# Eight of the 22 feature tiles of both down projections as Strassen block products

## The reference

```python
def swiglu(x, w_gate, w_up, w_down):
    return (jax.nn.silu(x @ w_gate) * (x @ w_up)) @ w_down

h = x + 0.5 * rmsnorm(swiglu(rmsnorm(h, ffn1_pre_g), ...), ffn1_post_g)
h = h + rmsnorm(hybrid_mixer(rmsnorm(h, mix_pre_g), ...), mix_post_g)
h = h + 0.5 * rmsnorm(swiglu(rmsnorm(h, ffn2_pre_g), ...), ffn2_post_g)
```

## Time and profile before

| | |
|---|---|
| median of 3 runs | 1090.79 us (1090.13 to 1091.5) |
| profiled execution, its own time | 1090.27 us |
| its span on the core | 1088.4 us, mean granted TensorE clock 1.000 |
| busy share of the span | PE 99%, DVE 61%, ACT 46%, POOL 4% |
| moved by DMA | 121.17 MB, mean 111 GB/s |

### The profile page before, as it was taken

One profiled execution on the slowest core, in us unless ns is written; L12 is line 12 of the kernel. 1 busy time (PEld: TensorE's weight loads), 2 busy tenths in 40 slices (PEclk: granted clock), 3 DMA queues, 4 the chain that ended last, 5 costly groups with the idle time before them and its releaser, 6 DMA issues.

```text
span 1088.4 us, 15986 instructions
## 1 busy us (share of the span) xinstructions
PE 1075.5 (99%) x6534; PEld 957.5 (88%) x6534; DVE 667.9 (61%) x810; ACT 503.0 (46%) x729; POOL 44.7 (4%) x96
## 2 busy tenths in 40 slices
PE   8999999999999999999999999999999999999997
PEld 6899999998888978888888888889899999988886
DVE  6898888873334663476664333468687887753334
ACT  7354455552223573667773222344445454542222
POOL 2000000000001210001000000011000000000001
PEclk9999999999999999999999999999999999999999
DMA  9522423334322544332115334315434234153311
GB/s 301 183 78 87 147 79 101 133 98 174 96 81 58 175 121 108 84 78 78 40 39 155 97 109 161 97 41 173 155 95 139 79 108 125 78 178 113 95 40 78
DMA packets 116131, 121.17 MB, mean 111 GB/s; under 512 B 6592, under 2 KB 100816, under 8 KB 116064
## 3 DMA queue, kind: packets, MB, share of 16 engines
q1 hardware_dynamic: 111744, 113.37, 33.8%
q10 hardware_dynamic: 3344, 4.20, 1.4%
q0 software_dynamic: 976, 2.66, 0.7%
HBM read 111.80 MB, written 6.29 MB: 108 GB/s over the span
## 4 chain that ended last, share of the span: by engine, by line
PE 90%; DVE 4%; ACT 3%; issue 1%; DMA 1%; POOL 0%; SPq 0%; ACTq 0%; DVEq 0%; POOLq 0%
PE bank L1448 25%; PE bank L1534 11%; PE bank L1536 11%; PE bank L1535 11%; PE bank L1438 7%; PE bank L1440 7%; PE bank L1439 7%; PE bank L1653 1%; PE bank L1654 1%; PE bank L1655 1%; PE bank L1503 1%; PE bank L1504 1%; PE bank L1505 1%; DMA raw<-in_ffn_w_up 1%; PE bank L1750 1%
## 5 line engine op out<-in xcount | busy, mean ns | idle before, releaser
L1534 PE MATMUL bank<-tc,w_hi 128*128 128x256 f32 x576 | 163.0, 283 | 0.0
L1535 PE MATMUL bank<-tc,w_hi 128*128 128x256 f32 x576 | 163.0, 283 | 0.0
L1536 PE MATMUL bank<-tc,w_lo 128*128 128x256 f32 x576 | 163.0, 283 | 0.0
L945 DVE TENSOR_TENSOR w_lo<-raw,w_hi 128x1024 fp32r<-128x1024 f32 x71 | 86.6, 1221 | 96.5 <-ACT w_hi L532 96.4
L1059 DVE TENSOR_TENSOR w_lo<-raw,w_hi 128x1024 fp32r<-128x1024 f32 x40 | 49.0, 1226 | 129.6 <-ACT w_hi L610 129.6
L1448 PE MATMUL bank<-w_hi,a_hi 128*128 128x512 f32 x408 | 126.1, 390 | 0.0
L1448 PE MATMUL bank<-w_hi,a_lo 128*128 128x512 f32 x408 | 125.7, 389 | 0.0
L1448 PE MATMUL bank<-w_lo,a_hi 128*128 128x512 f32 x408 | 125.6, 389 | 0.0
L1438 PE MATMUL bank<-u_hi,w_hi 128*128 128x512 f32 x312 | 124.0, 397 | 0.2 <-issue 0.2
L1534 PE MATMUL bank<-u_hi,w_hi 128*128 128x256 f32 x432 | 122.3, 283 | 0.8 <-DVE scr L1072 0.8
L1536 PE MATMUL bank<-u_hi,w_lo 128*128 128x256 f32 x432 | 122.2, 283 | 0.0
(11 more groups left out here) (244 smaller groups left out, 2057.9 us busy)
## 6 DMA issues: line engine op xcount, KB each, us to landing
raw<-in_ffn_w_down SPq DMA_DIRECT2D x40, 512.0 KB, 3.6
raw<-in_w_in SPq DMA_DIRECT2D x40, 512.0 KB, 3.8
h<-in_ffn_w_gate SPq DMA_DIRECT2D x9, 1024.0 KB, 5.5
h<-in_ffn_w_up SPq DMA_DIRECT2D x9, 1024.0 KB, 8.5
raw<-in_ffn_w_gate SPq DMA_DIRECT2D x9, 1024.0 KB, 5.4
raw<-in_ffn_w_up SPq DMA_DIRECT2D x9, 1024.0 KB, 8.0
h<-in_x SPq DMA_DIRECT2D x8, 512.0 KB, 6.5
h_store<-h SPq DMA_DIRECT2D x2, 2048.0 KB, 9.3
```

Source lines behind the costliest of these rows:

```text
L945: V.tensor_tensor(w_lo[:, slot(u), :], raw[:, slot(u), :], w_hi[:, slot(u), :].bitcast(F32), ALU.subtract).then_inc(lo_ready, 1)
L1534: mm(dst, w_hi[:, slot(u), w], moving(n, 0, k), start=first and k == 0, stop=False, skip_group_check=True)
L1535: mm(dst, w_hi[:, slot(u), w], moving(n, 1, k), start=False, stop=False, skip_group_check=True)
L1536: last = mm(dst, w_lo[:, slot(u), w], moving(n, 0, k), start=False, stop=k == KD // 2 - 1, skip_group_check=True)
```

## The change

The hidden tiles 0 to 7 and their 1024 rows of `w_down` are multiplied as 2 x 2 blocks (tokens x features by features x columns) with seven products instead of eight. Each product takes two units of 12 matmuls (`block_product`), so the eight tiles make 14 units (`BLOCK_UNITS`) and the projection 28 (`DOWN_UNITS`). DVE makes four sums of weights (`block_weights`, two halves each), in place, and three sums in PSUM (`block_quads`) of a bank and a snapshot that ACT took (`block_snapshot`). POOL makes the four sums of hidden tiles, two early (`act_sums_early`) and two in the block (`act_sums_late`); their places and the snapshots lie over `u_hi` and `u_lo`. Two extra matmuls open the banks of the fourth result, whose content DVE then writes. Tiles 8 to 21 are added plainly into the same banks. The block's weights are loaded as four quarters of 1 MB, two where the last pair but one lay, two where the last pair lay; the plain tiles' loads begin when all 14 units are split. `h` is reloaded by one DMA in both layers.

The diff's core:

```diff
+BLOCK_TILES = 8
+BLOCK_UNITS = 2 * STEPS
+DOWN_UNITS = BLOCK_UNITS + KF - BLOCK_TILES
+FFN_UNITS = 4 * CLASSIC + STEPS * QP + DOWN_UNITS
...
+DY, DX, DW, DZ = (1, 3), (0, 2), (4, 6), (5, 7)
+D_BANKS = (DY, DW, DY, DX, DY, DW, DY)
+D_QUARTER = ("11", "12", "11", "21", "12", "21", "22")
+D_SUM = {1: 1, 2: 3, 4: 5, 5: 7}
...
+        act_2 = u_place[:, 0, 0:4, TOK:N]
+        ACT_PLACES = (hidden_quarter(0, 0), hidden_quarter(1, 0), act_2, hidden_quarter(0, 1), hidden_quarter(0, 0),
+                      hidden_quarter(1, 1), hidden_quarter(0, 1))
+        ACT_SUM = {1: 1, 2: 2, 4: 3, 6: 4}
...
-                for n in range(KF):
-                    if n < SLOTS:
-                        sp.wait_ge(lo_ready, str_unit(layer, QP - 2, STEPS))
...
+                def block_load(name, k0, k1, done):
...
+                    sp.dma_start(dst[:, k0:k1, :], kmajor(wd[rows, :], cols)).then_inc(block_in[done], 16)
+                sp.wait_ge(lo_ready, str_unit(layer, QP - 2, STEPS))
+                block_load("11", 0, 4, "early")
+                block_load("22", 0, 4, "early")
+                sp.wait_ge(lo_ready, str_unit(layer, QP - 1, STEPS))
+                block_load("12", 0, 2, "12a")
+                block_load("12", 2, 4, "12b")
+                block_load("21", 0, 4, "21")
+                for n in range(BLOCK_TILES, KF):
+                    if n < BLOCK_TILES + SLOTS:
+                        sp.wait_ge(lo_ready, U_DOWN[layer] + BLOCK_UNITS)
...
-                        sp.wait_ge(lo_ready, U_DOWN[layer] + n - SLOTS + 1)
-                    if n == 2 * SLOTS and layer:
+                        sp.wait_ge(lo_ready, U_DOWN[layer] + down_unit(n) - SLOTS + 1)
+                    if n == BLOCK_TILES + SLOTS and layer:
                         sp.dma_start(h[:, :, :], h_store).then_inc(h_back, 16)
-                    elif n == 2 * SLOTS:
-                        for t in range(TT):
-                            sp.dma_start(h[:, t, :], x[t * P:(t + 1) * P, :]).then_inc(x_back[t], 16)
+                    elif n == BLOCK_TILES + SLOTS:
+                        sp.dma_start(h[:, :, :], x.rearrange("(t p) d -> p t d", p=P)).then_inc(h_back, 16)
...
-            def down_hi(layer, n):
-                u = U_DOWN[layer] + n
+            def block_hi(layer, d):
+                u, (n, half) = U_DOWN[layer] + d, divmod(d, 2)
+                if n in D_SUM:
+                    act.wait_ge(w_sum, block_sums(layer) + D_SUM[n] + half)
+                else:
+                    act.wait_ge(*((block_in["21"], 16 * (layer + 1)) if n == 3 else (block_in["early"], 32 * (layer + 1))))
+                act.wait_ge(unit_used, u - SLOTS + 1)
+                nc.scalar.activation(w_hi[:, slot(u), :], down_half(layer, D_QUARTER[n], half), ACT.Copy).then_inc(hi_ready, 1)
+                if n in ACT_SUM:
+                    act.wait_ge(act_sum, 4 * layer + ACT_SUM[n])
+                else:
+                    act.wait_ge(hidden_ready, PAIRS + 2 * CLASSIC * (layer + 1))
+                    act.wait_ge(quad_hidden, 3 * (layer * QP + 2))
+                nc.scalar.activation(a_slot(a_hi, u), act_half(n, half), ACT.Copy).then_inc(a_hi_ready, 1)
+                if half and 5 <= d <= 9:
+                    block_snapshot(layer, (d - 5) // 2)
...
+                act.wait_ge(unit_used, U_DOWN[layer] + 2 * n + 2)
+                for tt in range(2):
+                    last = nc.scalar.activation(block_snaps(n)[tt], bank[:, (DY, DW, DY)[n][tt], :], ACT.Copy)
+                last.then_inc(snap_done, 1)
...
+            def down_hi(layer, d):
+                if d < BLOCK_UNITS:
+                    return block_hi(layer, d)
+                n, u = d - BLOCK_UNITS + BLOCK_TILES, U_DOWN[layer] + d
...
-            def down_lo(layer, n):
-                u = U_DOWN[layer] + n
+            def block_weights(layer, name, half):
...
+                if name == "T3":
+                    dve.wait_ge(block_in["early"], 32 * (layer + 1))
+                    dve.wait_ge(block_in[("12a", "12b")[half]], 16 * (layer + 1))
+                    out, x, y, op = r12, r22, r12, ALU.subtract
+                elif name == "T2":
+                    dve.wait_ge(w_sum, block_sums(layer) + 1 + half)
+                    dve.wait_ge(lo_ready, d0 + half + 1)
+                    out, x, y, op = r11, r12, r11, ALU.add
+                elif name == "T1":
+                    dve.wait_ge(w_sum, block_sums(layer) + 3 + half)
+                    dve.wait_ge(lo_ready, d0 + 2 + half + 1)
+                    out, x, y, op = r12, r22, r11, ALU.subtract
+                else:
+                    dve.wait_ge(w_sum, block_sums(layer) + 3 + half)
+                    dve.wait_ge(lo_ready, d0 + 6 + half + 1)
+                    out, x, y, op = r21, r21, r11, ALU.subtract
+                V.tensor_tensor(out, x, y, op).then_inc(w_sum, 1)
...
+            def block_lo(layer, d):
+                u, (n, half) = U_DOWN[layer] + d, divmod(d, 2)
+                dve.wait_ge(hi_ready, u + 1)
+                V.tensor_tensor(w_lo[:, slot(u), :], down_half(layer, D_QUARTER[n], half),
+                                w_hi[:, slot(u), :].bitcast(F32), ALU.subtract).then_inc(lo_ready, 1)
+                dve.wait_ge(a_hi_ready, A_FFN[layer] + d + 1)
+                V.tensor_tensor(a_slot(a_lo, u), act_half(n, half), a_slot(a_hi, u).bitcast(F32),
+                                ALU.subtract).then_inc(a_lo_ready, 1)
...
+            def block_quads(layer, n):
+                snap, dst, src = ((0, DX, DX), (1, DZ, DY), (2, DW, DW))[n]
+                dve.wait_ge(unit_used, U_DOWN[layer] + 2 * n + 8)
+                dve.wait_ge(snap_done, parts(layer, QP) + (1, 3, 3)[n])
+                for tt in range(2):
+                    last = V.tensor_tensor(bank[:, dst[tt], :], block_snaps(snap)[tt], bank[:, src[tt], :], ALU.add)
+                last.then_inc(quad_ready, 1)
+            def down_lo(layer, d):
+                if d < BLOCK_UNITS:
+                    block_lo(layer, d)
+                    for name, half in {3: (("T2", 0), ("T2", 1)), 4: (("T1", 0),), 5: (("T1", 1),), 6: (("T4", 0),),
+                                       7: (("T4", 1),)}.get(d, ()):
+                        block_weights(layer, name, half)
+                    if d in (11, 13):
+                        block_quads(layer, (d - 11) // 2)
+                    return
+                n, u = d - BLOCK_UNITS + BLOCK_TILES, U_DOWN[layer] + d
...
-                split_a(A_FFN[layer] + n, u, arena[:, n, :])
+                split_a(A_FFN[layer] + d, u, arena[:, n, :])
+                if d == BLOCK_UNITS + 1:
+                    block_quads(layer, 2)
...
-                def down(k, i=0, first=False):
-                    weights(ud + k, i, 4)
-                    pe.wait_ge(a_lo_ready, i * 4 + (a0 + k + 1))
+                def block_product(d):
+                    n, half = divmod(d, 2)
+                    if d == 0:
+                        pe.wait_ge(quad_ready, parts(layer, QP - 1) + 1)
+                        pe.wait_ge(quad_hidden, 3 * (layer * QP + QP - 1))
+                    elif d == 2:
+                        pe.wait_ge(quad_hidden, 3 * (layer + 1) * QP)
+                    elif d == 4:
+                        pe.wait_ge(snap_done, parts(layer, QP) + 1)
+                    elif d == 8:
+                        pe.wait_ge(snap_done, parts(layer, QP) + 3)
+                    elif d == 12:
+                        pe.wait_ge(quad_ready, parts(layer, QP) + 2)
+                    weights(ud + d)
+                    pe.wait_ge(a_lo_ready, a0 + d + 1)
+                    s = slot(ud + d)
...
+                    for tt in range(2):
+                        dst = bank[:, D_BANKS[n][tt], :]
+                        for kk in range(2):
+                            toks = slice(kk * TOK + tt * P, kk * TOK + (tt + 1) * P)
+                            cols = slice(kk * HALF, (kk + 1) * HALF)
+                            start = n in (0, 1, 3) and half == 0 and kk == 0
+                            mm(dst, a_hi[:, s, toks], w_hi[:, s, cols], start=start, stop=False, skip_group_check=True)
+                            mm(dst, a_hi[:, s, toks], w_lo[:, s, cols], start=False, stop=False, skip_group_check=True)
+                            last = mm(dst, a_lo[:, s, toks], w_hi[:, s, cols], start=False, stop=False,
+                                      skip_group_check=True)
+                    if d == 2:
+                        for tt in range(2):
+                            last = mm(bank[:, DZ[tt], :], a_hi[:, s, 0:P], w_hi[:, s, 0:HALF], start=True, stop=False,
+                                      skip_group_check=True)
+                    last.then_inc(unit_used, 1)
...
+                def down(d, i=0):
+                    weights(ud + d, i, 4)
+                    pe.wait_ge(a_lo_ready, i * 4 + (a0 + d + 1))
                     for t in (0, 1, 3, 2):
-                        if first and t == 2:
```

(65 more changed lines are left out.)

72 lines of the change are left out of this document (46 added, 26 removed).

## The result

The changed kernel takes 1093.67 us (median of 9 runs, 1092.05 to 1095.02) against 1090.31 for the kernel before (9 runs, 1090.02 to 1091.5): 1.003 times as long, 95% interval 1.0021 to 1.0039. That is slower by 3.4 us, just over the 2.2 that a measurement here can tell from no change. The forecast was 1092.3 us by case A, "the path is held both ways". An engine is *held* while another one keeps it from working, and its *reserve* is how far it may be put back before PE has to wait for it.

What follows compares the result with a forecast made beforehand. PE, busy 99% of the span, was taken to bound the kernel: 1090.27 - 9.97 for 44 fewer matmuls + 12.0 lost to POOL's sums holding DVE and a late snapshot = 1092.3 us; range over the cases 1080 to 1098.

Steps and rivals of the forecast that it cites:

- case A: DVE and POOL block each other on the read path; sums of 1.7 to 2.6 us; 1088.4 to 1095.6; chance 0.45.
- DVE has no reserve: whatever holds it in the block holds PE: Block, layer 0: DVE ends its second block sum at 32.9 us, PE asks for it at 33.1.
- 2h - 0.2: Layer 0's block: us lost at unit 12 when two POOL sums, each h long, hold DVE.
- 2h - 1.8: Layer 1's block: us lost from two sums of length h, after 0.7 falls into DVE's waits before unit 3.
- a hair late: Layer 0's block: first snapshot ready at 11.4, PE's unit 4 wants it at 11.3; 0.15 us lost.
- case D: Sums take 2.6 to 2.9 us; waits at the seventh product and units 4, 8, 12; up to 1098.0; chance 0.13.
- The length: One 128x1024 sum on POOL from two SBUF operands: 2.2 us, bounds 0.97 and 2.9.
- Who comes first holds the path: Shared DVE and POOL read path: whichever engine starts first blocks the other; POOL sums up to 1.2 us longer.
- The early losses: PE waits for DVE at the third pair's seventh product: 3.2 us in layer 0, 1.9 in layer 1.
- The block losses: PE waits for DVE in the block: 4.2 us in layer 0, 2.6 in layer 1, plus 0.15 for the snapshot.
- none is priced: A clock fall during PE's stalls would come on top; the rows show none, so no time was added.
- The loads: Block and plain-tile loads stay hidden; unit 14's split has 0.6 us to spare; a 6.0 us load would cost 1.8 per layer.

Runs made afterwards that it cites:

- the sums are thin: Changed kernel with all eight GpSimd sums cut to the first of their 256 columns per tile: 1080.84 us.
- The sums on DVE: Changed kernel with all eight sums made by VectorE instead of GpSimd, at the same moments and into the same places: 1087.11 us.
- the half sums: Changed kernel with early GpSimd sums on 128 of 256 columns per tile and late sums cut to one column per tile: 1082.07 us.
- the sums at another moment: Changed kernel with all GpSimd sums early, one in each of pairs 3 to 6, released at VectorE's idle stretch: 1080.31 us.
- early thin: Changed kernel with only the two early sums per layer cut to one column per tile: 1086.27 us.
- late thin: Changed kernel with only the two block sums per layer cut to one column per tile: 1088.69 us.
- before with sums: Kernel before plus two whole GpSimd sums per layer after the second Strassen pair, their result read by nothing: 1097.53 us.

## Why the prediction was right, point by point

Case A came true, with luck in the size. The range over all cases, 1080 to 1098, was wide; "slower" had been given 0.29, less than "faster" with 0.44; and the sum of 1092.3 itself lay in the band of no change, which reached to 1093.0. The measured 1093.67 lies above it by errors that partly cancelled:

*The gain* was right: 6490 matmuls are left, and 9.44 of the 9.97 us show when the sums are thin.

*"DVE has no reserve: whatever holds it in the block holds PE"* was right, and stricter than its numbers. Without the sums DVE ends its second block sum in layer 0 at 268.89 + 1.29 = 270.18, 33.0 behind the block's first matmul at 237.16, where 32.9 were worked out. But 2h - 0.2 and 2h - 1.8 were worked out for the last deadline, unit 12. The sums on DVE showed that the nearer ones count, units 4 and 8, with 0.3 of reserve at layer 1's unit 4. Unit 4 had been seen as "a hair late", by 0.15 (0.33 measured), but the sum charges the held time at unit 12 alone; only case D names units 4 and 8.

*The length* h, put at 2.2, measured 2.39 where nothing is in the way, within the range of case A. (The Trainium skill, GPSIMD Engine Reference, 3.1, states 4497 ns for 2048 columns; half of it, 2.25 us as an estimate, is 0.14 below the 2.39 of this trace. By it the prediction's own sum would be 1092.75; its 1092.6 leaves out the 0.15.)

*The path held both ways*, of which the earlier trace rows showed one direction only, is shown: by the stretched operations, by their return in the kernel before with nothing added but the sums, by the half sums, and by 1080.31 with the sums at another moment. (The Trainium skill, SBUF — State Buffer, "Summary: rules for kernel authors", says of DVE operations with two SBUF inputs beside a GpSimd operation that reads SBUF that the second one to issue fully blocks. The trace agrees with 1.94 and 2.21 us in DVE's direction. It doesn't agree for the last sum: POOL issued at 261.26, and DVE's operations issued after it went first, for 6 us.)

*"Who comes first holds the path"* failed for that last sum. A wait of up to 1.2 behind DVE had been allowed for; the last sums waited 6.1 us in layer 0 and 7.9 in layer 1. In layer 1 ACT waited 2.79 us for the sum. By luck this cost next to nothing on top: ACT's copy was done at 1000.69, and DVE, held by the same sum until 1001.11, could not have used it before.

*The early losses*, forecast as 3.2 and 1.9, measured 3.05 and 2.04 of wait. Two errors cancelled. In layer 0 DVE was held for 4.15 (1.94 + 2.21), not 4.4, and its reserve was 0.99, not 1.23, since the wait that was counted as 0.24 lies ahead of the held operation. In layer 1 the two were 3.6 and 1.44, not 4.4 and 2.46, since the 1.02 lies ahead too.

*The block losses*, forecast as 4.2 + 0.15 and 2.6, measured 4.55 and 1.5. In layer 0 the total is right, but its place isn't: 2.3 at unit 4 and 1.6 by the clock, which left unit 12 with a wait of 0.17. In layer 1 DVE was held for 1.00 and 1.02 only (2.23 and 2.24 us for operations of 1.23 and 1.22), since the rest of both sums ran while it waited or worked with an operand in PSUM.

*The clock* is the term that was mis-sized: "none is priced". A lower clock cost 1.6 in layer 0's block, where the wait at unit 12 shrank to 0.17 for it, and 1.5 after layer 1's early wait, where it came on top. Term by term the loss is 13.0 where 12.05 was forecast: 1.5 more by this clock, 1.1 less in layer 1's block, 0.5 more by the rest. Three runs of the changed kernel have a mean clock of 0.998 and lie at 1092.05 to 1092.28, on the forecast and inside the 0.2%; the six with 0.995 to 0.997 lie at 1093.63 to 1095.02. That fits fewer falls in the three, but only one run has a trace, and mean clocks of 0.997 stand beside kernels whose traces have no such fall too.

*The loads* were hidden, as said: PE waited for none, and unit 14's split ended at 282.54, 0.44 before PE began with it (0.6 forecast). A tighter deadline stands behind it and is not in the prediction: the third block sum, on DVE behind the split of unit 15, is wanted by PE in the middle of unit 14. In the changed kernel it ended at 285.49, 0.2 before that. DVE and PE there, each a view of its own:

```profile
284.20 1.29 DVE L1180 TENSOR_TENSOR bank<-u_place,bank 128x512 f32<-128x512 f32 x2
```

```profile
285.70 0.63 PE L1587 MATMUL bank<-w_hi,a_hi 128*128 128x512 f32 x2
```

In the version with sums on DVE this is where unit 14 lost 0.77. ACT had waited 1.32 us for the load of unit 15's weights, the third block sum ended at 282.09, and PE waited for it:

```profile
282.14 0.73 PE L1606 MATMUL bank<-w_hi,a_hi 128*128 128x512 f32 x2 [0.61 <-DVE bank L1194]
```

Left open: why DVE lets POOL in at 106.1 and at 245.5, between two operations that follow closely, and not between 261.3 and 267.5. One thing sets the places apart in the rows: at the first two the DVE operation that POOL sat behind had itself come out of a wait (the 0.48 and the 0.17 above); at 261.3 it had not. Whether that decides was not tested.

## What to carry to other kernels

Before work is given to GpSimd because it is idle, look at what VectorE does at that moment. Here operations with two SBUF operands on the two engines took turns, and up to the whole length of a sum (2.39 us) landed on one VectorE operation. Release such work where VectorE waits for someone else; here that was worth 13 us (1093.67 to 1080.31), once there were free places for two of the sums. And work out a reserve for each deadline on the way, counting only the waits that lie behind the held operation.

## What the hardware showed unexpectedly

- In this case GpSimd was kept out by a VectorE stream without a gap: a sum of four columns took 8.07 us, in both layers, and 2.86 and 2.87 once VectorE stopped for its own last operation. At other moments GpSimd got in between two close operations; what decides is open (above).
- In four kernels (changed, early thin, late thin, before with sums) eight of these waits of TensorE were 2.0 to 3.1 us long. After five of them the granted clock fell, to 0.57 over the worst 4 us each time (254.25 to 258.25 in the changed kernel), and about 1.5 us more were lost; after three it didn't. The wait of 3.05 in layer 0 was followed by a fall with the late sums thin and by none in the changed kernel. After the waits of up to 1.24 us that the sums caused in the other kernels it never fell. What decides was not found.
- The clock row of the page did not show these falls: of a slice of 27 us they are too small a part. Windows of 4 us do.
